# A two-layer hybrid trunk with mixture of experts on Trainium2: token rows scattered as quarters, the last down unit by output tile, one activation table loaded earlier

## The reference

```
xn = rms_norm(h, g)                        # h * rsqrt(mean(h*h) + 1e-6) * g
q, k, v, u, h_conv, b, c, gates = split(xn @ w_in)   # 1024 x 5632
merged = sig(gA) * (attention(q,k,v) @ w_br_a) + sig(gB) * (s5(u) @ w_br_b) + sig(gC) * (conv(...) @ w_br_c)
h = h + merged @ w_out
layer 0:  h = h + (silu(xn @ w_gate) * (xn @ w_up)) @ w_down          # 1024 -> 3584 -> 1024
layer 1:  logits = xn @ w_router; top 2 of 8 experts, softmax of the two logits
          h = h + sum over the two experts of share * swiglu_e(xn)     # each 1024 -> 3584 -> 1024
```

## Time and profile before

| what | us |
|---|---|
| median of 3 runs (lowest, highest) | 1611.92 (1610.66, 1616.89) |
| the profiled execution | 1612.83 |
| its span, first to last instruction | 1611.1 |
| TensorE busy in the span | 1572.2 |
| VectorE, ScalarE, GpSimd busy | 546.8, 355.5, 247.8 |

### The profile page before, as it was taken

The page is one execution under the profiler, slowest core; times in us unless marked ns, Lnnn a source line. Parts: engine busy times, 40 slices in busy tenths (PEclk is TensorE's granted clock), DMA queues, the critical chain, the costliest instruction groups (busy, mean ns, idle before and its releaser), DMA issues.

```text
span 1611.1 us, 30918 instructions
## 1 busy us (share of the span) xinstructions
PE 1572.2 (98%) x14095; PEld 945.6 (59%) x14095; DVE 546.8 (34%) x751; ACT 355.5 (22%) x437; POOL 247.8 (15%) x301
## 2 busy tenths in 40 slices
PE   7999999999998999999999999999999999999997
PEld 6978999999998988984333333333333333333322
DVE  6887567544445577562101110111011001110111
ACT  5442344444445451440000000000000000000001
POOL 3437279100000166000000000000000000000023
PEclk9999999999999999999999999999999999999999
DMA  9722488755555502759999999999999999999994
GB/s 276 236 79 79 128 269 316 243 183 184 184 183 165 175 27 79 247 212 394 419 419 393 419 419 386 419 404 404 420 386 420 420 392 420 417 393 420 402 402 200
DMA packets 154180, 484.58 MB, mean 301 GB/s; under 512 B 10912, under 2 KB 95904, under 8 KB 139712
## 3 DMA queue, kind: packets, MB, share of 16 engines
q1 hardware_dynamic: 147664, 467.30, 76.0%
q10 hardware_dynamic: 4816, 10.04, 1.7%
q0 software_dynamic: 1568, 5.24, 0.9%
HBM read 467.22 MB, written 15.34 MB: 300 GB/s over the span
## 4 chain that ended last, share of the span: by engine, by line
PE 91%; DVE 4%; DMA 2%; ACT 1%; issue 1%; SPq 1%; ACTq 0%; DVEq 0%
PE work L702 30%; PE work L1017 17%; PE acc L1034 17%; PE acc L1017 11%; PE ssm_y L1017 6%; PE acc L702 5%; DMA ring<-in_moe_w_down 2%; PE work L815 1%; PE ssm_y L822 1%; SPq L589 1%; PE work L723 1%; DVE arena L1381 0%; PE acc L785 0%; DVE parts L1363 0%; DVE xs L1370 0%
## 5 line engine op out<-in xcount | busy, mean ns | idle before, releaser
L702 PE MATMUL work<-xs,parts 128*128 128x256 f32 x3648 | 462.5, 287 | 12.9 <-DVE xs L1370 10.2
L702 PEld LDWEIGHTS work<-xs,parts 128*128 128x128 f32 x3648 | 449.9, 194 | 24.3 <-issue 19.3
L1017 PE MATMUL work<-ring,arena 128*32 128x448 f32 x3072 | 312.3, 539 | 0.3 <-DVE arena L1667 0.2
L1034 PE MATMUL acc<-ring,arena 128*32 128x512 f32 x2688 | 291.9, 592 | 4.6 <-DMA ring<-in_moe_w_down 4.6
L1363 DVE TENSOR_TENSOR parts<-ring,parts 128x2048 fp32r<-128x2048 f32 x94 | 218.6, 2329 | 152.6 <-ACT parts L1113 152.4
L1705 DVE TENSOR_TENSOR arena<-arena,work 128x448 f32<-128x448 f32 x48 | 26.9, 616 | 594.0 <-ACT arena L1288 594.0
L1017 PE MATMUL acc<-ring,arena 128*32 128x448 f32 x2048 | 216.2, 539 | 0.8 <-ACT arena L1288 0.8
L1017 PEld LDWEIGHTS work<-ring,arena 128*32 128x32 f32 x3072 | 100.9, 110 | 188.4 <-issue 186.4
L1034 PEld LDWEIGHTS acc<-ring,arena 128*32 128x32 f32 x2688 | 87.1, 110 | 205.6 <-issue 191.7
L1113 ACT ACTIVATE parts<-ring 128x2048 fp32r<-128x2048 f32 x94 | 179.2, 1909 | 120.7 <-PE work L702 66.7
L1288 ACT ACTIVATE arena<-acc 128x448 f32<-128x448 f32 x32 | 15.7, 542 | 664.0 <-PE work L1017 664.0
(11 more groups left out here) (295 smaller groups left out, 982.8 us busy)
## 6 DMA issues: line engine op xcount, KB each, us to landing
ring<-in_moe_w_gate SPq DMA_DIRECT2D x128, 896.0 KB, 20.4
ring<-in_moe_w_up SPq DMA_DIRECT2D x128, 896.0 KB, 20.9
ring<-in_moe_w_down SPq DMA_DIRECT2D x112, 1024.0 KB, 23.1
ring<-in_w_in SPq DMA_DIRECT2D x44, 1024.0 KB, 6.5
ring<-in_dense_w_gate SPq DMA_DIRECT2D x14, 1024.0 KB, 5.1
ring<-in_dense_w_up SPq DMA_DIRECT2D x14, 1024.0 KB, 5.3
ring<-in_dense_w_down SPq DMA_DIRECT2D x14, 1024.0 KB, 5.0
routed<-arena ACTq DMA_DIRECT2D x1, 9216.0 KB, 31.8
```

The source lines that it names most:

```text
L702: last = nc.tensor.matmul(out_ap, a, b, start=start and n == 0, stop=stop and n == len(pairs) - 1, skip_group_check=shared)
L1017: last = nc.tensor.matmul(banks[g][GRP * q:GRP * q + GRP, 0:CHUNK], x, w[:, q * CHUNK:q * CHUNK + CHUNK], start=k == 0, stop=k == KT - 1, ...
L1034: last = nc.tensor.matmul(acc[GRP * q:GRP * q + GRP, b, :], eh[:, which, 2 * u + kk, g * GRP:g * GRP + GRP], w[:, kk, half * OUT_COLS:half ...
```

## The change

It has five parts. First, `routed` is also seen as quarters of rows (`routed_quarters`, rows of 256 numbers). DVE computes four quarter indices per token and choice from its place (quarter index = 384 x block + 96 x quarter + 3 x slot within a group of 32 + group), and POOL scatters sixteen times 128 quarters of 1 KB, in place of four times 128 rows of 4 KB. Second, a block of rows is then loaded with one DMA, 128 partitions with one run of 3 KB each; the first of these loads is moved behind the block ("d", 0, 0). Third, the last dense down unit runs with the output tiles outside, and `down_banks` signals each finished bank, for which DVE's residual adds wait one by one. Fourth, the table set with Ln and Exp is requested on ACT behind the last Silu of the dense layer. Fifth, TensorE issues nine products of 128 columns into the unused `ssm_y` bank behind layer 1's first sum of squares.

```diff
--- before.py
+++ after.py
@@ -206,7 +206,9 @@
             self.bank = self.n % WB
             self.done = self.n + 1
 
+    XQ = D // 4
     routed = nc.dram_tensor("routed", [CAND * SLOTS, D], F32).ap()
+    routed_quarters = routed.rearrange("r (f d) -> (r f) d", d=XQ)
 
     ctx = ExitStack()
     with ctx:
@@ -322,6 +324,9 @@
         counts = carve(NE)
         listf = carve(CAND + 3)
         total = carve(NE)
+        block_of_place = carve(2 * TT).rearrange("p (c t) -> p c t", t=TT)
+        group_of_place = carve(2 * TT).rearrange("p (c t) -> p c t", t=TT)
+        quarter_at = carve(2 * TT * 4).rearrange("p (c t q) -> p c t q", t=TT, q=4)
         sumsq = carve(2 * TT).rearrange("p (t c) -> p t c", c=2)
         first_half = carve(TT)
         from_last = carve(2 * TT).rearrange("p (c t) -> p c t", t=TT)
@@ -335,6 +340,7 @@
         late_squares = cosT
         items = sb("items", [P, CAND + 3], I32)
         places = sb("places", [P, 2, TT], I32)
+        quarters = sb("quarters", [P, 2, TT, 4], I32)
         zeros = kT.rearrange("p t n -> p (t n)")
         y_late = hT[:, :, :].rearrange("p k n -> p (k n)").rearrange("p (t n) -> p t n", n=D)
 
@@ -404,6 +410,7 @@
         half_done = sem("half_done")
         br_full = sem("br_full")
         down_done = sem("down_done")
+        down_banks = sem("down_banks")
         xs_hi_ready = sem("xs_hi_ready")
         xs_ready = sem("xs_ready")
         hid_hi_ready = sem("hid_hi_ready")
@@ -420,6 +427,7 @@
         xe_ready = sem("xe_ready")
         x_rows_loaded = sem("x_rows_loaded")
         places_ready = sem("places_ready")
+        quarters_ready = sem("quarters_ready")
         routed_stored = sem("routed_stored")
         y_left = sem("y_left")
         y_moved = sem("y_moved")
@@ -512,6 +520,8 @@
         def used_up(l, name):
 
             n = int(name[-1]) if name[0] not in "GUD" else int(name[1:])
+            if name == f"D{NHC - 1}":
+                return down_banks, KT // 2
             if name[0] == "D":
                 return down_done, n + 1
             if name[0] == "G":
@@ -592,14 +602,10 @@
                 if not isinstance(i, int) or i > 1:
                     sp.wait_ge(xe_ready, i - 1)
                 else:
-                    sp.wait_ge(routed_stored, 16 * 2 * TT)
-                block = (routed[c * SLOTS:c * SLOTS + SLOTS, :] if isinstance(c, int) else
-                         routed.rearrange("(c s) d -> c s d", s=SLOTS)[bass.ds(c, 1), :, :]
-                         .rearrange("a s d -> (a s) d"))
-                for q in range(4):
-                    sp.dma_start(x_rows[GRP * q:GRP * q + GRP, :].rearrange("p (g n) -> p g n", g=NG),
-                                 block[:, q * XC4:q * XC4 + XC4].rearrange("(g s) n -> s g n", g=NG))\
-                        .then_inc(x_rows_loaded, 16)
+                    sp.wait_ge(routed_stored, 16 * 2 * TT * 4)
+                blocks = routed_quarters.rearrange("(c p g) n -> c p (g n)", p=P, g=NG)
+                block = (blocks[c:c + 1, :, :] if isinstance(c, int) else blocks[bass.ds(c, 1), :, :])
+                sp.dma_start(x_rows, block.rearrange("a p n -> (a p) n")).then_inc(x_rows_loaded, 16)
 
             def store_rows(i, c):
                 sp.wait_ge(y_high, i + 1)
@@ -632,7 +638,7 @@
             for n in range(2, LOOP_AT):
                 kind, which, i = BLOCKS[n][:3]
                 waited = load_block(n, i, waited)
-                if BLOCKS[n] == ("gu", 1, i, 0):
+                if BLOCKS[n] == (("gu", 1, i, 0) if i else ("d", 0, i)):
                     load_rows(i + 1, i + 1)
                 if BLOCKS[n] == ("d", 0, i) and i:
                     store_rows(i - 1, i - 1)
@@ -703,6 +709,12 @@
                                             stop=stop and n == len(pairs) - 1, skip_group_check=shared)
                 return last
 
+            def idle_products(n):
+
+                for i in range(n):
+                    nc.tensor.matmul(ssm_y[:, 0, 0:P], neg_ones[:, :], ident[:, :], start=True, stop=True,
+                                     skip_group_check=True)
+
             def sum_squares(l, part):
                 g = Group(("rms", l, part))
                 bank = begin(g)
@@ -723,6 +735,8 @@
                     last = nc.tensor.matmul(bank[:, 0:L], neg_ones[:, :], xnT[:, k, :], start=k == 0,
                                             stop=k == KT - 1)
                 last.then_inc(work_done, 1)
+                if l:
+                    idle_products(9)
 
             pe.wait_ge(consts_made, 4)
             for t in range(KT * TT // 4):
@@ -892,13 +906,25 @@
                 def dense_down_product(c):
                     w = weights(0, f"D{c}")
                     pe.wait_ge(hid_split, (c + 1) * FT)
+
+
+                    def tile(f, n):
+                        pairs = three(w, [h_parts[:, c % 2, q, f, :] for q in range(2)],
+                                      (slice(0, P), f, slice(n * P, n * P + P)), slice(0, P))
+                        return accumulate(acc[:, n // 2, (n % 2) * L:(n % 2) * L + L], pairs,
+                                          start=c == 0 and f == 0 and n % 2 == 0,
+                                          stop=c == NHC - 1 and f == FT - 1, shared=True)
+
+                    if c == NHC - 1:
+                        for n in range(KT):
+                            for f in range(FT):
+                                last = tile(f, n)
+                            if n % 2:
+                                last.then_inc(down_banks, 1)
+                        return
                     for f in range(FT):
                         for n in range(KT):
-                            pairs = three(w, [h_parts[:, c % 2, q, f, :] for q in range(2)],
-                                          (slice(0, P), f, slice(n * P, n * P + P)), slice(0, P))
-                            last = accumulate(acc[:, n // 2, (n % 2) * L:(n % 2) * L + L], pairs,
-                                              start=c == 0 and f == 0 and n % 2 == 0,
-                                              stop=c == NHC - 1 and f == FT - 1, shared=True)
+                            last = tile(f, n)
                     last.then_inc(down_done, 1)
 
                 for c in range(NHC):
@@ -1246,6 +1272,7 @@
                         if c:
                             splits.upto(0, f"D{c - 1}")
                     hidden_high(DENSE_TILES - 1)
+                    act.preload_act_table_set("natural_log_exp_and_others")
                     splits.upto(0, f"D{NHC - 1}")
 
             act.dma_start(g_row, gain_final[0:1, :].to_broadcast([P, D])).then_inc(row_loaded, 16)
@@ -1593,8 +1620,8 @@
                             splits.upto(0, f"D{c - 1}")
                     hidden_rest(DENSE_TILES - 1)
                     splits.upto(0, f"D{NHC - 1}")
-                    dve.wait_ge(down_done, NHC)
                     for b in range(4):
+                        dve.wait_ge(down_banks, b + 1)
                         tt(hT[:, 2 * b:2 * b + 2, :].rearrange("p t n -> p (t n)"),
                            hT[:, 2 * b:2 * b + 2, :].rearrange("p t n -> p (t n)"), acc[:, b, :], ALU.add)\
                             .then_inc(h_ready, 1)
@@ -1670,6 +1697,20 @@
 
             move_half(Group(("gather0", 1)))
 
+            for floors, size in ((block_of_place, SLOTS), (group_of_place, GRP)):
+                link(ts(floors[:, :, :], ends[:, :, :], -(size - 1) / 2.0, 1.0 / size, ALU.add, ALU.mult))
+                link(ts(floors[:, :, :], floors[:, :, :], magic, None, ALU.add))
+                link(ts(floors[:, :, :], floors[:, :, :], -magic, None, ALU.add))
+            link(ts(quarter_at[:, :, :, 0], ends[:, :, :], float(NG), None, ALU.mult))
+            link(stt(quarter_at[:, :, :, 0], group_of_place[:, :, :], float(1 - NG * GRP), quarter_at[:, :, :, 0],
+                     ALU.mult, ALU.add))
+            link(stt(quarter_at[:, :, :, 0], block_of_place[:, :, :], float(4 * SLOTS - NG), quarter_at[:, :, :, 0],
+                     ALU.mult, ALU.add))
+            for q in range(1, 4):
+                last = ts(quarter_at[:, :, :, q], quarter_at[:, :, :, 0], float(q * SLOTS), None, ALU.add)
+            link(last)
+            nc.vector.tensor_copy(quarters[:, :, :, :], quarter_at[:, :, :, :]).then_inc(quarters_ready, 1)
+
             dve.wait_ge(expd_ready, 1)
             link(ts(stat[:, :, 4:5], stat[:, :, 3:4], 1.0, None, ALU.add))
             link(nc.vector.reciprocal(stat[:, :, 5:6], stat[:, :, 4:5]))
@@ -1709,7 +1750,7 @@
                                     erow[:, :].rearrange("p (g i f) -> p f g i", g=NG, f=FTILES)).then_inc(eh_ready, 1)
 
             def turn_rows(i, first_slot):
-                dve.wait_ge(x_rows_loaded, i * 64)
+                dve.wait_ge(x_rows_loaded, i * 16)
                 nc.vector.transpose(xe[:, :, first_slot:first_slot + SLOTS].rearrange("p f (g n) -> p f g n", g=NG),
```

(9 more changed lines are left out.)

## The result

The changed kernel takes 1601.62 us (median of 5, 1601.23 to 1603.28) and the kernel before, run beside it, 1612.52 (5 runs): a ratio of 0.9933 [0.9919, 0.9948]. The profiled execution took 1601.6 us with a span of 1599.8, so 11.3 us of span have gone. The gain is small, 0.7%, but the interval lies clear of 1. Run again in a later set, it gave 1602.02 against 1613.66, 0.9929 [0.9915, 0.9942].

A forecast was written before the change was run, and what follows sets the result against it. TensorE was taken to bound nearly everywhere, with DMA also full in the expert stage. Gains of 1.25 + 1.28 + 1.5 + 6.4 = 10.4 us from a median of 1611.92 gave 1602; range 1599.5 to 1610.

The forecast's parts named there:

- Down unit by tile: Last dense down unit: with output tiles outside, the sum of squares ends at 492.97 instead of 494.22, gaining 1.25 us.
- Table load: Seam before layer 1: the load ahead of Exp moves into ACT's idle time, gaining 1.28 us.
- Clock: TensorE at layer 1's first q product: idle products leave no gap over 0.5 us, keeping the clock up, gaining 1.5 us.
- rival 2: Seam: the clock falls anyway or the idle products run long, 1.5 or 1.7 us less gain, 1604; chance 0.11.
- Expert stage: Last expert item: full-width row loads lose almost no DMA rate, so TensorE's 6.4 us of waiting for weights come back.
- Rival 1: Expert stage: row loads stay slow because of the HBM tensor or small packets, about 1610 us; chance 0.18.
- The scatter is free: Start of expert stage: quarter scatter costs 0, since the row load moved behind the down loads spares SP 19 us of holding.
- POOL's 16 issues unbroken: Scatter: indices ready at 728.95, 16 issues at 1.34 us until 750.4, last landing 13.3 later, at 764.
- Rival 3: Scatter: software queue doesn't hold 16 scatters; at two at a time TensorE stands 35 us, 1637 us; chance 0.06.
- POOL's closing adds: End of kernel: they end at 1586.4, needed at 1592.5, so they don't bind.
- What would show it: Signs in the profile: no table load at L1141, L723 at 489.3, clock 1.00, landings under 20 us, no weight or scatter waits.
- windows at 410 or more: Expert stage sign: DMA rate in the windows around the row loads reaches at least 410 GB/s; near 380 would disprove.

The follow-up runs named there:

- rows only: The changed kernel without the old-to-new seam edits (down unit by tile, early table load, idle products): 1606.92 us, ratio 0.9956 to the kernel before.
- no idle products: The changed kernel without TensorE's nine idle products ahead of layer 1's first product: 1602.95 us, ratio 0.9931 to the kernel before.
- no idle products, no early load: The changed kernel without the nine idle products and without the early table load on ACT: 1617.24 us, ratio 1.0027 to the kernel before.
- after: The kernel before with all five parts of the change: 1601.62 us, and 1602.02 us when run again unedited in a later set.

## Why the prediction was right, by its steps

1602 was forecast and 1601.62 measured; the mechanism was the likeliest one of the text, and the terms forecast at 10.4 came to 2.83 + 1.28 + 6.17 = 10.28. That the number agrees within 0.4 is partly luck. 0.94 us of the span came from a part that nothing was forecast for, and the start of the last down unit, where it shows, lies anywhere from 476.57 (rows only) to 478.11 (no idle products) in other runs.

- **Down unit by tile.** 1.25 predicted. 1.55 by the kernel with the old order, and 2.83 - 1.28 = 1.55 in the traces. The term was short by 0.3: the sum doesn't only start earlier, it also takes 3.48 without the wait ahead of it.
- **Table load.** 1.28 predicted, 1.29 measured (no idle products, no early load).
- **Clock.** 1.5 predicted, 1.28 measured; in the two other kernels with a gap of 3.8 us the low clock cost 1.5 and 2.7, so the size could have come out otherwise. The step named a wrong cause: the idle products were said to hold the clock, but the gap shortened from 3.8 to 2.5 us does, by the run without them. At 2.17 us they are as long as forecast and useless, and rival 2 had no case: without them the clock stayed as well.
- **Expert stage.** 6.4 predicted, 6.17 measured; the width was the cause, by 3.0 and 3.2 us a load narrow against 0.1 and 0.4 wide, as far as four wide DMAs, which were not run, leave it. Rival 1 is refuted: it named the tensor or small packets, and the wide load of 1 KB runs reads the same tensor at 416. The Trainium skill's rule (page "SBUF — State Buffer", section Door 1: The DMA port swizzle) points at the right cause. The prediction's estimate from it, 0.9 us a load, is less than a third of what the narrow loads lost here, because it counts only the rows' own packets. Most of the loss falls on the weights beside them (2.0 of 2.5 us in the window taken apart above).
- **The scatter is free.** On SP it was, but "the move is what makes the scatter free" failed: at the old place SP was held 14.0 us (19 predicted) and the time was 1600.88. I priced a held SP as if the loads had no lead, though I had used that lead for the backlog.
- **POOL's 16 issues unbroken.** They came as 14 and 2, with 6.7 us between. The indices were ready at 723.57, on a scale 5 us earlier than the 728.95 forecast, so as predicted. At the old place the rows were all stored at 752.35, where 764 - 5 = 759 had been forecast: the last landings took less than 13.3. Rival 3, a queue too small, did happen at 14 and at 7, and cost nothing on SP: even with 7 the stores were long done when SP asked. What such a queue touches instead, TensorE's supply, no rival had.
- **POOL's closing adds** were to stay where they were, against the earlier trace rows. The last began 26.7 us earlier:

```profile
1557.34 2.38 POOL L1954 TENSOR_TENSOR arena<-arena,hT 128x1024 f32<-128x1024 f32 x1
```

The stores they wait for no longer stand behind a backlog. It binds nothing.
- **What would show it.** All signs came: no table load at Exp, the sum right behind the down unit, clock 1.00, landings under 20, no wait of TensorE for weights. Only "windows at 410 or more" was put badly: the last shows 402 since nothing is asked for.

## What to carry to other kernels

When a long balanced stage loses its DMA rate at certain transfers, add up the deficit and look at which partitions they write: four 96 KB loads to 32 partitions each slowed the weights beside them here, and the gain lay in the shape, not in the packet size. Before filling a gap of TensorE with idle work, see whether the gap, once shortened, still drops the clock. Costing a held queue, set it against what has been loaded ahead. And with many indirect DMAs beside dense matmuls, look at TensorE's timeline itself, as busy shares and waits show hardly a shortage of instructions.

## What the runs showed of the hardware that was not expected

- TensorE issuing one to four matmuls at a time, with pauses of 0.2 to 1.5 us, while POOL issues indirect DMAs in a row: 13.4 us lost with 14 in a row, 5.4 with 7, in seven of the twelve kernels run with quarter scatters, after counted twice.
- The software queue took 14 indirect DMAs of 128 rows with a room of 2048 and 7 with 1152. Behind the first such row POOL stood idle for 6.5 to 6.8 us, but only for 2.1 to 3.0 in the five kernels with the long shortage, in which the DMA had less to do. Within a row one issue came about every 1.27 us.
- The granted clock stayed at 1.00 over a gap of 2.5 us and fell to 0.50 to 0.60 behind gaps of 3.8; that cost TensorE 1.3, 1.5 and 2.7 us in three kernels.
- Four loads of 32 partitions in a full DMA stream lost 3.0 to 3.2 us in all per 384 KB; the same bytes in one load to 128 partitions 0.1 to 0.4. While the narrow ones moved, the weights' own packets took longer as well (299 ns against 276 over 30 us).
